# Recurrent pairs of a two-part transformer: 128-wide block-diagonal matrices replaced by compact 64 by 64 blocks

## The reference, cut to what matters

```python
def step(S, inp):
    r_t, w_t, k_t, v_t, a_t, b_t = inp
    sa = jnp.einsum('bhvk,bhk->bhv', S, a_t)
    S = S * w_t[:, :, None, :] + sa[..., None] * b_t[:, :, None, :] + v_t[..., None] * k_t[:, :, None, :]
    return S, jnp.einsum('bhvk,bhk->bhv', S, r_t)
...
xs = (seq_first(r), seq_first(decay), seq_first(k), seq_first(v), seq_first(-kk), seq_first(kk * a))
_, y = lax.scan(step, jnp.zeros((B, H, N, N), f32), xs)
```

## Time and profile before

| | us |
|---|---|
| median of 3 runs | 3558.96 (3557.36 to 3561.98) |
| the profiled run | 3558.77 |
| its span, first to last instruction | 3556.6 |
| TensorE busy | 3296.5 (93%) |
| VectorE, ScalarE, GpSimd busy | 1909.6, 1186.1, 198.6 |
| mean granted TensorE clock | 0.968 of full speed |

### The profile page before, as it was taken

How to read it: one execution, slowest core, us unless ns; L and a number is a source line. 1 busy time by engine, 2 the same in 40 slices (tenths; PEclk the granted TensorE clock), 3 DMA queues, 4 the chain that set the end, 5 groups by cost and what they waited for, 6 DMA issues and landing times.

```text
span 3556.6 us, 37068 instructions
## 1 busy us (share of the span) xinstructions
PE 3296.5 (93%) x14704; PEld 2573.5 (72%) x14704; DVE 1909.6 (54%) x2822; ACT 1186.1 (33%) x1849; POOL 198.6 (6%) x173
## 2 busy tenths in 40 slices
PE   9969897999989997899989989999999989999999
PEld 6648785778767775688756748878877656878887
DVE  4664435424357775533357664564556756456463
ACT  4332223313134343423235332332334423243232
POOL 0114210000000001000000000000001000010000
PEclk9989898999999999999999989999999989999999
DMA  4110001222211211122221112222223111222322
GB/s 167 60 48 1 16 1 48 88 91 93 79 73 60 72 60 53 66 95 95 83 91 65 66 37 94 95 95 89 98 77 106 61 59 59 95 92 86 100 90 76
DMA packets 41543, 264.81 MB, mean 74 GB/s; under 512 B 4600, under 2 KB 4984, under 8 KB 13980
## 3 DMA queue, kind: packets, MB, share of 16 engines
q1 hardware_dynamic: 41364, 262.44, 21.5%
q10 hardware_dynamic: 8, 0.01, 0.0%
HBM read 260.33 MB, written 3.42 MB: 74 GB/s over the span
## 4 chain that ended last, share of the span: by engine, by line
PE 70%; DVE 8%; ACT 4%; issue 2%; SPq 0%; DVEq 0%; ACTq 0%
PE psum L336 21%; PE psum L337 21%; PE psum L338 21%; DVE w_lo L318 1%; ACT tiles L938 1%; PE psum L917 1%; PE psum L1893 1%; PE psum L1894 1%; PE psum L1895 1%; PE psum L761 1%; PE psum L908 1%; DVE tiles L963 1%; PE psum L1805 1%; DVE tiles L1697 1%; ACT xT L792 1%
## 5 line engine op out<-in xcount | busy, mean ns | idle before, releaser
L336 PE MATMUL psum<-hi,w_hi 128*128 128x512 f32 x3672 | 1480.7, 403 | 76.9 <-SPq L431 28.2
L337 PE MATMUL psum<-lo,w_hi 128*128 128x512 f32 x3672 | 1460.3, 398 | 0.0
L338 PE MATMUL psum<-hi,w_lo 128*128 128x512 f32 x3672 | 1458.8, 397 | 0.0
L336 PEld LDWEIGHTS psum<-hi,w_hi 128*128 128x128 f32 x3672 | 695.3, 189 | 262.2 <-issue 72.8
L318 DVE TENSOR_TENSOR w_lo<-ring,w_hi 128x1024 fp32r<-128x1024 f32 (+1 forms) x495 | 604.4, 1221 | 470.5 <-ACT w_hi L310 469.8
L310 ACT ACTIVATE w_hi<-ring 128x1024 fp32r<-128x1024 f32 (+1 forms) x495 | 505.1, 1021 | 982.2 <-PE psum L338 921.2
L337 PEld LDWEIGHTS psum<-lo,w_hi 128*128 128x128 f32 x3672 | 695.8, 189 | 170.0 <-issue 5.6
L338 PEld LDWEIGHTS psum<-hi,w_lo 128*128 128x128 f32 x3672 | 694.6, 189 | 170.4
L726 DVE SCALAR_TENSOR_TENSOR xT<-xT,psum 128x512 f32<-128x512 f32 x96 | 66.1, 688 | 238.9 <-PE psum L338 238.9
L938 ACT ACTIVATE tiles<-tiles,small 128x256 f32<-128x256 f32 (+3 forms) x176 | 95.0, 541 | 166.6 <-DVE small L963 166.0
L1573 DVE TENSOR_TENSOR tiles<-tiles 128x512 f32<-128x512 f32 x64 | 44.3, 692 | 180.6 <-ACT tiles L1565 180.6
(11 more groups left out here) (256 smaller groups left out, 2968.9 us busy)
## 6 DMA issues: line engine op xcount, KB each, us to landing
ring<-in_weights SPq DMA_DIRECT2D x211, 1024.0 KB, 4.8
ring<-in_weights SPq DMA_DIRECT2D x28, 704.0 KB, 4.0
ring<-in_weights SPq DMA_DIRECT2D x4, 896.0 KB, 4.5
held<-in_const SPq DMA_DIRECT2D x2, 1344.0 KB, 8.4
ring<-in_weights SPq DMA_DIRECT2D x3, 832.0 KB, 4.4
xT<-in_x SPq DMA_DIRECT2D x8, 256.0 KB, 5.5
tiles<-bias_repeated SPq DMA_DIRECT2D x8, 256.0 KB, 5.1
out<-xT SPq DMA_DIRECT2D x8, 256.0 KB, 2.1
```

What stands on the lines that cost most here:

```text
L336: pe.matmul(out, hi, rhs.hi(first + at), start=(at == 0), stop=False)
L337: pe.matmul(out, hi, rhs.lo(first + at), start=False, stop=False)
L338: last = pe.matmul(out, lo, rhs.hi(first + at), start=False, stop=(at == total - 1))
```

## The change

All matrices become compact: a tile of 128 partitions and 512 columns has, for chunk c, the 64 by 64 block of one head in its lower and of the other in its upper partitions, at columns 64c to 64c+63. One tile so holds what took two. `small_products` multiplies block by block: 64 partitions, 64 stationary and 64 moving columns, first all chunks of the lower head and then all of the upper. In `invert` the two halves of a level are now chunks 0 to 3 and 4 to 7 of both heads in place of the two heads. The four transposes become products with a 64 by 64 identity. The state is 128 partitions by 64 columns, the cleared tiles and their copies go, and `matrices` has three ticks in place of four. The masks in the constants are 64 columns wide, with the first load of constants 512 columns shorter. A pair uses 10 tiles in place of 15. Where the diff shows no removed line, the line before is in the code above.

```diff
 COMMON = [("ident", P), ("mean", P), ("mean64", P), ("sum64", P), ("eps", 4)]
-FIRST = [("cos", T), ("sin", T), ("reset", T), ("low0", P)] + \
-    [(f"up{l}", P) for l in range(LEVELS)] + [("up", P), ("upincl", P)]
+FIRST = [("cos", T), ("sin", T), ("reset", T), ("low0", CHUNK), ("one", CHUNK)] + \
...
+            put("low0", low[:, 0:CHUNK] | low[:, CHUNK:P])
+        put(f"up{l}", low.T[:, 0:CHUNK] | low.T[:, CHUNK:P])
+    row, col = a % CHUNK, b[:, 0:CHUNK]
+    put("one", row == col)
+    put("up", row < col)
+    put("upincl", row <= col)
...
-    return tile.rearrange("p (i t) -> p i t", i=TB)
+    return tile.rearrange("p (c t) -> p c t", t=CHUNK)
...
-def spread(mask):
-    return mask.unsqueeze(1).to_broadcast([P, TB, P])
+def spread(mask, n=NCHUNK):
+    return mask.unsqueeze(1).to_broadcast([P, n, CHUNK])
...
+def at_chunk(c):
+    return slice(c * CHUNK, (c + 1) * CHUNK)
+def small_products(pe, out, left, right, chunks=range(NCHUNK)):
+    for h in range(2):
+        for c in chunks:
+            last = pe.matmul(out[HALF[h], at_chunk(c)], left[HALF[h], at_chunk(c)], right[HALF[h], at_chunk(c)],
+                             start=True, stop=True)
+    return last
...
+        self.tokA, self.tokB, self.tokK, self.tokV, self.X, self.XT, self.NT, self.AK, self.level, self.av = \
+            (k.tile(work + n) for n in range(10))
+        self.RB, self.RK, self.TA = self.X, self.NT, self.level
+        self.SA, self.states = self.tokA, self.AK
         self.banks = [k.bank(bank + b) for b in range(4)]
     def S(self, n):
+        return self.states[:, at_chunk(n)]
...
+                    for c in range(NCHUNK):
+                        for h in range(2):
+                            last = pe.matmul(bank[HALF[h], at_chunk(c)], src[HALF[h], at_chunk(c)],
+                                             k.c("ident")[HALF[h], HALF[h]], start=True, stop=True)
                     last.then_inc(made, 1)
             if t == 1:
                 pe.wait_ge(act_done, 1)
...
+                small_products(pe, b4[2], kt, at).then_inc(made, 1)
             if t == 2:
                 pe.wait_ge(act_done, 4)
+                pe.wait_ge(dve_done, 2)
+                small_products(pe, b4[3], AK, self.tokV).then_inc(made, 1)
...
+            if t == 1:
+                act.wait_ge(made, 6)
+                act.activation(NT, b4[1], ACT.Copy).then_inc(act_done, 1)
...
+            if t == 1:
+                dve.wait_ge(made, 5)
+                dve.tensor_tensor(blocks(X), blocks(b4[0]), spread(k.c("low0")), ALU.mult).then_inc(dve_done, 1)
+                dve.wait_ge(made, 7)
+                dve.tensor_tensor(blocks(AK), blocks(b4[2]), spread(k.c("up")), ALU.mult).then_inc(dve_done, 1)
+                dve.wait_ge(dve_done, 1)
+                dve.tensor_tensor(blocks(X), blocks(X), spread(k.c("one")), ALU.add).then_inc(x_ready, 1)
...
+            if t == 1:
+                pool.wait_ge(act_done, 5)
+                pool.tensor_tensor(blocks(XT), blocks(NT), spread(k.c("up0")), ALU.mult).then_inc(xt_ready, 1)
+                pool.wait_ge(xt_ready, 1)
+                pool.tensor_tensor(blocks(XT), blocks(XT), spread(k.c("one")), ALU.add).then_inc(xt_ready, 1)
...
         level_ready, p_done, p_copied, xp_done, x_ready = (k.sem() for _ in range(5))
         X, XT, NT, PR, level = self.X, self.XT, self.NT, self.AK, self.level
+        part = [slice(0, T // 2), slice(T // 2, T)]
+        own = [range(0, NCHUNK // 2), range(NCHUNK // 2, NCHUNK)]
...
+            if l >= 2:
+                pool.wait_ge(p_done, 2 * (l - 1))
+            pool.tensor_tensor(blocks(level), blocks(NT), spread(k.c(f"up{l}")), ALU.mult).then_inc(level_ready, 1)
...
+                pe.wait_ge(self.m["x_ready"], 1)
+                pe.wait_ge(self.m["xt_ready"], 2)
+                pe.wait_ge(self.m["act_done"], 6)
+            pe.wait_ge(level_ready, l)
+            for g in range(2):
                 if l >= 2:
+                    pe.wait_ge(x_ready, n - 2 + g + 1)
+                small_products(pe, bank(l, g, "p"), level, X, own[g]).then_inc(p_done, 1)
+            for g in range(2):
+                pe.wait_ge(p_copied, n + 2)
                 if l < LEVELS - 1:
+                    small_products(pe, bank(l, g, 0), XT, PR, own[g])
+                small_products(pe, bank(l, g, 1), PR, XT, own[g]).then_inc(xp_done, 1)
...
+                act.wait_ge(p_done, 2 * t + g + 1)
                 if l >= 2:
+                    act.wait_ge(xp_done, 2 * (t - 1) + g + 1)
+                act.activation(PR[:, part[g]], bank(l, g, "p")[:, part[g]], ACT.Copy).then_inc(p_copied, 1)
...
+            for g in range(2):
+                w = part[g]
+                dve.wait_ge(xp_done, 2 * t + g + 1)
                 if l < LEVELS - 1:
+                    dve.tensor_tensor(X[:, w], X[:, w], bank(l, g, 0)[:, w], ALU.add)
+                dve.tensor_tensor(XT[:, w], XT[:, w], bank(l, g, 1)[:, w], ALU.add).then_inc(x_ready, 1)
...
+                small_products(pe, b4[0], self.tokA, self.XT).then_inc(ta_done, 1)
+                small_products(pe, b4[1], self.XT, self.av).then_inc(tv_done, 1)
...
+                small_products(pe, b4[2], self.bt, self.rt).then_inc(made, 1)
+                small_products(pe, b4[3], self.kt, self.rt).then_inc(made, 1)
...
+        cleared, sa_done, sa_ready, state_done, state_ready = (k.sem() for _ in range(5))
+        SA, S, tokV = self.SA, self.S, self.tokV
+        self.c = dict(sa_ready=sa_ready, state_ready=state_ready)
...
                 pool.memset(S(0), 0.0).then_inc(cleared, 1)
...
+            c = at_chunk(n)
             if n == 0:
+                pe.wait_ge(cleared, 1)
+                pe.wait_ge(self.a["masked"], 2)
                 pe.wait_ge(self.a["copied"], 2)
             if n >= 1:
                 pe.wait_ge(state_ready, n)
             if n >= 2:
                 pe.wait_ge(sa_ready, n - 1)
+            for h in range(2):
+                last = pe.matmul(b4[n % 2][HALF[h], 0:CHUNK], self.TA[HALF[h], c], S(n)[HALF[h], :], start=True, stop=True)
+            last.then_inc(sa_done, 1)
             if n == NCHUNK - 1:
                 return
+            out = b4[2 + n % 2]
+            for h in range(2):
+                pe.matmul(out[HALF[h], 0:CHUNK], k.c("ident")[HALF[h], HALF[h]], S(n)[HALF[h], :], start=True, stop=False)
+            for h in range(2):
+                pe.matmul(out[HALF[h], 0:CHUNK], self.tokK[HALF[h], c], tokV[HALF[h], c], start=False, stop=False)
             pe.wait_ge(sa_ready, n + 1)
+            for h in range(2):
+                last = pe.matmul(out[HALF[h], 0:CHUNK], self.tokB[HALF[h], c], SA[HALF[h], c], start=False, stop=True)
+            last.then_inc(state_done, 1)
...
+            dve.tensor_tensor(SA[:, c], self.av[:, c], b4[n % 2][:, 0:CHUNK], ALU.add).then_inc(sa_ready, 1)
...
+            dve.tensor_scalar(S(n + 1), b4[2 + n % 2][:, 0:CHUNK], self.fexp[:, n:n + 1], None, ALU.mult).then_inc(state_ready, 1)
+        return Work(NCHUNK, tensor, None, vector, gpsimd)
...
+        y, sq, rstd = self.key, self.XT, self.level
...
+                for n in range(NCHUNK):
+                    c = at_chunk(n)
                     for h in range(2):
+                        pe.matmul(b4[0][HALF[h], c], self.SA[HALF[h], c], self.RB[HALF[h], c], start=True, stop=False)
+                    for h in range(2):
+                        pe.matmul(b4[0][HALF[h], c], self.tokV[HALF[h], c], self.RK[HALF[h], c], start=False, stop=False)
+                    for h in range(2):
+                        last = pe.matmul(b4[0][HALF[h], c], self.S(n)[HALF[h], :], self.rt[HALF[h], c], start=False, stop=True)
                 last.then_inc(y_done, 1)
             if t == 1:
                 pe.wait_ge(y_copied, 1)
...
```

More of the change, by code:

```diff
@@ L519, in load_first @@
     sp.dma_start(k.common[:, :], const_in[:, 0:at]).then_inc(k.common_loaded, 16)
-    sp.dma_start(k.held[:, :], const_in[:, at:end]).then_inc(k.first_loaded, 16)
+    sp.dma_start(k.held[:, 0:end - at], const_in[:, at:end]).then_inc(k.first_loaded, 16)
     sp.dma_start(k.mask[:, :], mask_in[:, 0:T]).then_inc(k.mask_loaded, 16)
@@ L1233, in matrices @@
         self.m = dict(act_done=act_done, x_ready=x_ready, xt_ready=xt_ready)
[L1235 to L1239, removed]
         def tensor(pe, t):
@@ L1253, in tensor @@
                 pe.wait_ge(act_done, 1)
-                outer(pe, b4[0], at, bt, 0)
+                small_products(pe, b4[0], at, bt).then_inc(made, 1)
                 pe.wait_ge(act_done, 2)
-                outer(pe, b4[1], bt, at, 0)
+                small_products(pe, b4[1], bt, at).then_inc(made, 1)
                 pe.wait_ge(act_done, 3)
-                outer(pe, b4[2], kt, at, 0)
+                small_products(pe, b4[2], kt, at).then_inc(made, 1)
             if t == 2:
                 pe.wait_ge(act_done, 4)
[L1261 to L1272, removed]
+                pe.wait_ge(dve_done, 2)
```

(29 more changed lines are left out.)

134 lines of the change are left out of this document (14 added, 120 removed).

## The result

The changed kernel takes 3493.91 us (median of 4 runs, 3493.06 to 3495.27) against 3558.16 of the kernel before beside it (3557.18 to 3561.98): 0.9818 of the time, interval 0.9801 to 0.9835. That is 64 us faster, where 5 were forecast, and outside the range of 3510 to 3585. The profiled run took 3494.08 us with a span of 3492.3; the span before was 3556.6, so the trace holds the same 64 us.

The account below looks back on a forecast made before the run. TensorE's order of instructions was taken to set 267 of the two stages' 284 us. Terms 8.1 + 2.9 - 13.1 + 1.9 - 8.7 + 3.5 summed to -5.4 us, say 3554 us; range 3510 to 3585.

Parts of the forecast that it names:

- I take 0.058: TensorE's small products: 0.058 us a record in a long stream, from bounds of 0.031 and 0.060, or 0.109 should nothing shrink.
- the array's 0.056: A 64 by 64 record in one corner of the array: about 0.056 us, from 0.109 with both sides halved.
- the five wrong terms of the table: Forecast changes over both stages: matrices +11.0, inversion -13.1, application +1.9, chunks -8.7, outputs +3.5 us.
- The 1.51 us of the earlier trace: Before the change: 16 records, 64 stationary and 128 moving columns, eight into each PSUM half, end pause included.
- rival (c): The array alone limits small products: records 0.046, 0.036 or 0.031 us, -69 us, 3490; chance 0.10.
- 0.031 to 0.058 in the earlier trace: TensorE's handing over of instructions after an emptied queue, held against rival (c); load and product together 0.058 to 0.060 us.
- The inversion: 16 levels at 5.67 us in place of 6.31, copy hidden, -10.2; last levels -2.9 us.
- Matrices: Both pairs of pairs 29.7 us, +8.1 and +2.9, GpSimd's chain ending about with TensorE; rival (c) gave -8.
- Chunks: Pair-chunk 1.0 us in place of 1.26, chain and sixteen records (0.93) both limiting; -8.7 us.
- rival (d): TensorE's granted clock at 1.2 GHz throughout the small-product stages: about +68 us, 3627; chance 0.10.
- the counts of records: Records of one pair after: matrices 256, inversion 96 a level and 64 last, application 128, chunks 116, outputs 96.
- the tail: Last 17.4 us of the two stages, reciprocals on VectorE, forecast to stay.

## Why the prediction was wrong

**The step that failed** is "I take 0.058": the time of a record in a long stream, set at the interval between two records after an emptied queue. That number was right for one corner (0.059) and so looked consistent with the array's 0.056, but it was applied to both corners one after the other. In four of the five wrong terms of the table it is the step itself, and in the chunks it is a part. Records took 0.030 (turning, outputs), 0.048 (groups of 16) and 0.040 (groups of 8). The prediction said 1 ns in a record moves the sum by 4 us; the 61 us between forecast and measurement are some 14 ns in the mean.

**The clue was there and was read.** The 1.51 us of the earlier trace rows were explained as two or three records beside the other half's; the runs measure about two and a half (0.048 and 0.040 us in groups of 16 and of 8, from 0.058) to three at each change. It was even carried to the end as rival (c), with 3490 us and records of 0.046, 0.036 and 0.031 us where 0.048, 0.040 and 0.030 were measured, and given one chance in ten. What spoke against it, 0.031 to 0.058 in the earlier trace rows, could not bear the weight: the 0.058 is an interval between loads of 128 by 128, and a small record's was not in the trace. Records of 64 by 64 followed each other in 0.016 us with four corners, so handing over limits nothing at 0.058; what held those two loads no run here tells. Handing over and array had one number, and I took the coincidence as support for both.

**The inversion**: 4.31 us for 5.67. The copy was not hidden, 0.47 us of TensorE's idle time stayed, which fits a level that is held by the array and not by dispatch; dispatch could have gone on during the wait. On the loads the gap is shorter than before, 0.61 us for the 0.88 of the earlier trace rows, as this row of the loads after has it:

```profile
296.58 3.70 PEld L1198 LDWEIGHTS psum<-tiles 64*64 64x64 f32 x96 [0.61 <-ACT tiles L1338]
```

So the shorter copy is worth up to 0.27 us of a level's 2.0; the rest is the records.

**Matrices**: TensorE was finished sooner than GpSimd's chain: it waits 0.62 us for the level's mask in the first stage, and 4.08 at the border of the second, where it waited 2.29 before. That keeps (c)'s -8 at -4.3.

**Chunks**: the pair-chunk is 0.845 us in place of the 1.0 forecast; VectorE's addition took 0.21 and its scaling 0.28, 0.22 each forecast, and the records were shorter. It is held by the chain in the given order and not by the 16 records, which take 0.46: TensorE waits 0.17 us for each addition, and with the other pair's records put in between (half ticks) it fell to 0.72.

**The clock**: rival (d) said the clock could fall. In the changed kernel it is 0.89 from 284 to 300, where the first level has 5.23 us in place of 3.84, and 0.91 over the second inversion, where it was 0.94. But the runs show it near: the same count of records in one corner, in one half of the rows, or in longer groups stood at 0.5 for tens of microseconds and cost from 14 us (turning in groups) to some 137 (one corner) more than the overlap explains. Its mechanism was put wrongly: not small products as such bring the clock down. In the stages read here it fell where TensorE had just waited, and with the order went how soon it was back: within 4 us in the changed kernel's first level, after 48 with longer groups and pauses, and not within the inversion with one corner or one half of the rows.

**Right** were the counts of records, the tail (17.39 for 17.36), and that nothing outside the two stages moves by more than about 1 us (64.3 us of the span against 65.3 in the stages, with an entry 0.8 us later). One slip in the prediction bears on little: 5.4 us for 48 records are 0.113 us each, not 0.111.

## What to carry to other kernels

Products of 64 by 64 that alternate between corners of the array cost half of those in one corner, so put the head (or whatever picks the corner) in the inner loop and the blocks in the outer one; four corners, here with two PSUM banks, nearly halve it again for as long as the stream lasts (151 records here). When two candidate limits give one number, look in the trace for a row where only one of them can hold, here products that change the corner. And count the granted clock as part of an order's price: behind a wait it came back late with long stays in one corner, and within some 10 us where heads with their own rows and columns changed often or the waits in the levels were hidden.

## What was not expected of the hardware

A TensorE without a pause can stay at a granted clock of 0.5: 45 us in one corner, and 45 us of groups of 16 (260.25 to 305), both of which began at the low clock; the same one-corner stream that began at 1.0 kept it for 33 us (with the clearing products between), until a wait. Turning products whose heads alternate in rows and columns were at 1.0 some 4 us after the same low start; those that alternate in columns alone stayed at 0.5. One kernel's runs can scatter by 45 us (3510 to 3555) on that alone. And a stream of 0.016 us a record ran dry after 151 records, for 1.46 us.
